# First block's mixers: gated output product with 128 output rows, splits behind chains, rotation on GpSimd, key squares on ScalarE

## The reference, cut to what matters

```python
# layer 0: q, k, v, a_low, r, q_mem = split(h @ gla_w_in); 4 heads, keys 128, values 256, 4 chunks of 64
scores  = einsum('bnhid,bnhjd->bnhij', qc * exp(bc - b_ref), kc * exp(b_ref - bc))     # causal in a chunk
o_intra = einsum('bnhij,bnhjv->bnhiv', scores, vc)
# state before chunk n: S_n = decay * S_(n-1) + (kc * exp(b_last - bc))^T vc,  S_0 = 0
o_inter = einsum('bnhid,bnhdv->bnhiv', qc * exp(bc), s_prev)
o = rmsnorm(o_intra + o_inter, gla_out_norm) * silu(r)
# layer 1: c_q, c_kv, k_r, q_mem = split(h @ mla_w_in)
q  = (rmsnorm(c_q) @ w_uq)  -> q_nope, q_rope;   kv = (rmsnorm(c_kv) @ w_ukv) -> k_nope, v     # 8 heads
q_rope = apply_rope(rmsnorm(q_rope), cos, sin)
# memory, both layers: k, v = split(rmsnorm(mem) @ mem_w_kv); k = rmsnorm(k); softmax attention, 4 heads
x = x + concatenate([o, o_mem]) @ w_out
```

## Time and profile before

| | us |
|---|---|
| median of 3 runs | 1778.82 |
| lowest, highest | 1773.97, 1779.57 |
| the profiled execution | 1773.2 |
| its span, first to last instruction | 1771.4 |

### The profile page before, as it was taken

One profiled execution on the slowest core, in us unless ns is written; L12 is line 12 of the kernel. 1 busy time (PEld: TensorE's weight loads), 2 busy tenths in 40 slices (PEclk: granted clock), 3 DMA queues, 4 the chain that ended last, 5 costly groups with the idle time before them and its releaser, 6 DMA issues.

```text
span 1771.4 us, 28082 instructions
## 1 busy us (share of the span) xinstructions
PE 1687.7 (95%) x10080; PEld 1470.2 (83%) x10080; DVE 1237.3 (70%) x1810; ACT 953.1 (54%) x1548; POOL 73.5 (4%) x78
## 2 busy tenths in 40 slices
PE   7999999899999999999699999997999998899998
PEld 6999987599999989987579899984788877578887
DVE  5876786347766787675766876758577668767765
ACT  5654553446555555555555654547455445755553
POOL 0100010000000000001200100000000001000000
PEclk9999999999999999999999999999999999999999
DMA  6666554244655456544415665550366654037652
GB/s 220 204 208 189 161 166 144 83 163 157 207 185 178 159 197 201 185 159 155 131 54 168 199 204 189 165 186 25 109 199 196 194 180 132 12 119 220 195 192 93
DMA packets 79329, 287.00 MB, mean 162 GB/s; under 512 B 8848, under 2 KB 9232, under 8 KB 79008
## 3 DMA queue, kind: packets, MB, share of 16 engines
q1 hardware_dynamic: 78336, 282.25, 49.6%
q0 software_dynamic: 608, 3.15, 0.5%
q10 hardware_dynamic: 320, 0.74, 0.1%
HBM read 285.05 MB, written 1.05 MB: 162 GB/s over the span
## 4 chain that ended last, share of the span: by engine, by line
PE 82%; DVE 8%; ACT 5%; DMA 3%; issue 2%; POOL 0%; SPq 0%; ACTq 0%; DVEq 0%; POOLq 0%
PE ps L1828 25%; PE ps L1832 13%; PE ps L1755 9%; PE ps L1800 6%; PE ps L1801 6%; PE ps L1802 6%; PE ps L1813 3%; DMA raw<-units 3%; PE ps L1814 3%; PE ps L1815 3%; PE ps L2164 2%; PE ps L2128 2%; DVE wlo L1097 2%; ACT whi L728 1%; PE ps L1915 1%
## 5 line engine op out<-in xcount | busy, mean ns | idle before, releaser
L1261 DVE TENSOR_TENSOR wlo<-raw,whi 128x1024 fp32r<-128x1024 f32 x380 | 463.7, 1223 | 122.7 <-ACT whi L857 122.0
L1828 PE MATMUL ps<-acts,whi 128*128 128x512 f32 x2016 | 505.9, 393 | 1.7 <-DVE prob L1268 1.0
L857 ACT ACTIVATE whi<-raw 128x1024 fp32r<-128x1024 f32 x380 | 398.2, 1051 | 94.8 <-PE ps L1832 63.9
L1828 PEld LDWEIGHTS ps<-acts,whi 128*128 128x128 f32 x2016 | 365.3, 189 | 69.6 <-DVE prob L1268 1.4
L1832 PEld LDWEIGHTS ps<-acts,wlo 128*128 128x128 f32 x2016 | 275.1, 190 | 19.7
L1097 DVE TENSOR_TENSOR wlo<-raw,whi 128x1024 fp32r<-128x1024 f32 x154 | 187.6, 1236 | 135.4 <-ACT whi L728 134.9
L1832 PE MATMUL ps<-acts,wlo 128*128 128x256 f32 x2016 | 281.1, 282 | 0.0
L728 ACT ACTIVATE whi<-raw 128x1024 fp32r<-128x1024 f32 x154 | 159.5, 1054 | 142.0 <-DMA raw<-units 105.7
L1755 PE MATMUL ps<-whi,acts 128*128 128x512 f32 (+1 forms) x708 | 210.5, 389 | 8.7 <-DVE wlo L1097 2.6
L1800 PE MATMUL ps<-hid_hi,wlo 128*128 128x256 f32 x704 | 199.3, 283 | 0.0
L1801 PE MATMUL ps<-hid_hi,whi 128*128 128x256 f32 x704 | 199.3, 283 | 0.0
(11 more groups left out here) (208 smaller groups left out, 2124.1 us busy)
## 6 DMA issues: line engine op xcount, KB each, us to landing
raw<-units SPq DMA_DIRECT2D x534, 512.0 KB, 4.1
arena<-mem_in POOLq DMA_DIRECT2D x2, 1024.0 KB, 7.9
x<-x_in SPq DMA_DIRECT2D x4, 256.0 KB, 6.2
arena<-mem_in POOLq DMA_DIRECT2D x4, 256.0 KB, 4.9
out<-x SPq DMA_DIRECT2D x4, 256.0 KB, 2.1
const<-const_in ACTq DMA_DIRECT2D x1, 560.0 KB, 5.3
row<-row_in ACTq DMA_DIRECT2D x1, 134.0 KB, 6.3
gain<-gain_in SPq DMA_DIRECT2D x1, 76.5 KB, 1.9
```

Source lines behind the costliest of these rows:

```text
L857: nc.scalar.activation(whi[:, u % RING, :], raw[:, u % RAW, :], ACT.Copy).then_inc(hi_ready, 1)
L1261: V.tensor_tensor(wlo[:, u % RING, :], raw[:, u % RAW, :], whi[:, u % RING, :].bitcast(F32), ALU.subtract).then_inc(lo_ready, 1)
L1828: T.matmul(ps[:, bank, :], whi[:, slot, w], acts[:, k].rearrange("p e s -> p (e s)"), start=k == 0, stop=False)
```

## The change

- **Output product.** `g_sT` becomes twice as wide: per token tile a 128x128 matrix with the two chunks' masked scores on its diagonal and zeros beside, written by one longer clearing and two predicated copies of 64 partitions. Each (tile, head) is one full product with v plus products with the states: one in tile 0 (the decayed queries of chunk 0 set to zero), two in tile 1 (queries of the one chunk with zeros for the other). GpSimd clears and copies these queries (`g_qx1`, in the place of the decayed keys once these are transposed); TensorE waits for it (`queries_apart`).
- **Squares and splits.** The product signals after each token tile, and ScalarE squares each at once, with one of its three splits moved behind the squares. The vector engine moves one split behind the gated products, and two behind the q_mem evacuation. The r projection does not wait for the qmT copies. The wait for the gated rows moves from before the memory attention to its first transposes of them.
- **Latent mixer.** Squares of the memory keys on ScalarE, with their sums on the vector engine later; kmT copied by ScalarE rather than the vector engine; the scaling of memory keys and `kn` in another order; rotation of `m_qr` by GpSimd, between the statistics of kn and qn; several splits moved; the latents' transposes two tiles later.

```diff
-SQUARED = {name: TT * (n + 1) for n, name in enumerate(("memq0", "memq1", "kn", "qn", "qr", "bq"))}
+SQUARED = {name: TT * (n + 1) for n, name in enumerate(("memq0", "memq1", "memk1", "kn", "qn", "qr", "bq"))}
...
+        g_sT = at_arena(G_S, 1024).rearrange("p (h t i) -> p h t i", h=GH, t=TT)
+        g_qx = arena3(G_QX, GH, S)
+        g_qx1 = at_arena(G_KD, 1024).rearrange("p (h e i) -> p h e i", h=GH, e=2)
+        QR_OUT = 5 + 6
```

GpSimd in the gated mixer:

```diff
-                    self.stats("memq0", "gla")
+                    self.stats("memq0")
+                    pool.wait_ge(gla_dve, 6)
+                    nc.gpsimd.memset(g_qx[:, :, 0:GC], 0.0).then_inc(queries_apart, 1)
+                    pool.wait_ge(turned, 4)
+                    nc.gpsimd.memset(at_arena(G_KD, 1024), 0.0).then_inc(zeroed, 1)
+                    pool.wait_ge(zeroed, 1)
+                    for e in range(2):
+                        nc.gpsimd.tensor_scalar(g_qx1[:, :, e, e * GC:(e + 1) * GC],
+                                                g_qx[:, :, P + e * GC:P + (e + 1) * GC], 1.0, None, ALU.mult
+                                                ).then_inc(queries_apart, 1)
+                    self.stats("gla")
```

GpSimd in the latent mixer:

```diff
-                    self.stats("memq1", "cq", "ckv", "kr", "memk1", "kn", "qn", "qr")
+                    self.stats("memq1", "cq", "ckv", "kr", "memk1", "kn")
+                    self.rotate_queries()
+                    self.stats("qn", "qr")
+                def rotate_queries(self):
+                    pool.wait_ge(evac_act, QR_OUT)
+                    pool.wait_ge(evac_dve, QR_OUT)
+                    for out_, e, k in ((a, 0, 0), (b, 1, 1), (c, 0, 2), (d, 1, 3)):
+                        tt(out_, v[:, :, :, e, :], tabs[k], ALU.mult).then_inc(rotated, 1)
+                    pool.wait_ge(rotated, 4)
+                    pool.wait_ge(squared, SQUARED["qr"])
+                    tt(v[:, :, :, 0, :], a, b, ALU.subtract).then_inc(rotated, 1)
+                    tt(v[:, :, :, 1, :], c, d, ALU.add).then_inc(rotated, 1)
```

ScalarE in the gated mixer:

```diff
-                    self.split(3)
-                    act.wait_ge(gla_pe, 6)
+                    self.split(2)
                     for t in range(TT):
+                        act.wait_ge(gla_pe, 6 + t)
                         for h in range(GH):
...
+                    self.split(1)
                     self.evacuate(4, vm, NARROW, "mem0")
```

ScalarE in the latent mixer:

```diff
                     self.evacuate(4, km, NARROW, "mem1")
-                    self.memory_keys(1)
+                    act.wait_ge(ss_dve, STAT["memq1"][1])
+                    self.squares_of(square_q, km)
                     self.split(1)
...
                     self.squares_of(rows, m_qn)
+                    self.take([(kmT[:, h, :], GAIN_AT["memk_norm"] + 1) for h in range(XH)])
                     self.split(2)
                     self.evacuate(2, m_qr, MIDDLE, "cq")
-                    self.split(2)
-                    act.wait_ge(ss_dve, STAT["memq1"][1])
+                    self.split(1)
+                    act.wait_ge(ss_dve, STAT["memk1"][1])
                     self.squares_of(square_q, m_qr)
                     self.split(2)
                     self.evacuate(2, m_v, CROSSED, "ckv")
                     self.take([(by_tile(m_krT), None)])
                     self.take([(by_tile(m_kT[:, h, :]), GAIN_AT["mla_kn_norm"]) for h in range(MH)])
-                    self.split(1)
+                    self.split(2)
```

The vector engine in the gated mixer:

```diff
-                        if dst in (G_KJ, G_KD):
-                            self.split(1 if dst == G_KJ else 2)
+                        if dst == G_KJ:
+                            self.split(1)
                     self.evacuate(4, qm, NARROW, "mix0")
-                    self.split(2)
+                    self.split(4)
...
                     self.evacuate(8, g_r, WIDE, "mix0")
-                    self.split(3)
+                    self.split(2)
                     dve.wait_ge(gla_act, 6)
...
                         ins.then_inc(rows_ready, 1)
+                    self.split(1)
                     self.evacuate(4, vm, NARROW, "mem0")
```

The vector engine in the latent mixer:

```diff
                     self.evacuate(4, km, NARROW, "mem1")
-                    self.memory_key_sums(1, rows)
                     self.split(1)
+                    self.evacuate(2, m_k, WIDE, "ckv")
+                    dve.wait_ge(squared, SQUARED["memk1"])
+                    self.sums_of("memk1", square_q, XH)
+                    self.split(1)
+                    dve.wait_ge(squared, SQUARED["kn"])
+                    self.sums_of("kn", rows, MH)
                     self.scale_memory_keys(1)
...
-                    self.evacuate(2, m_k, WIDE, "ckv")
-                    self.split(2)
-                    dve.wait_ge(squared, SQUARED["kn"])
-                    self.sums_of("kn", rows, MH)
+                    self.split(1)
                     self.evacuate(3, m_qn, CROSSED, "cq")
-                    self.memory_keys(1)
-                    self.split(2)
                     kn = m_k.rearrange("p t (h w) -> p t h w", h=MH)
                     self.scale_heads("kn", kn, kn, MH, NOPE).then_inc(rows_ready, 1)
+                    self.g += 2
+                    self.split(2)
                     self.evacuate(2, m_qr, MIDDLE, "cq")
-                    self.split(2)
                     dve.wait_ge(squared, SQUARED["qn"])
...
+                    self.split(1)
                     self.evacuate(2, m_v, CROSSED, "ckv")
-                    self.step(self.rotate(m_qr.rearrange("p t (h e c) -> p t h e c", h=MH, e=2),
-                                          [m_tab[:, 0, n] for n in range(4)], tmp))
-                    self.split(1)
+                    self.split(2)
                     self.g += 1 + 4 + 4
+                    dve.wait_ge(rotated, 6)
                     dve.wait_ge(ratio_ready, 2)
```

TensorE:

```diff
-                    self.project(range(KD), 1024, WIDE, between=beside)
+                    self.project(range(KD), 1024, WIDE, between=beside, taken=False)
                     def read():
+                        pe.wait_ge(queries_apart, 3)
...
-                                for e in range(2):
-                                    n = 2 * t + e
-                                    r = slice(e * GC, (e + 1) * GC)
-                                    o = ps_y[r, t, h * GDV:(h + 1) * GDV]
-                                    ins = T.matmul(o, g_sT[r, h, t, :], g_v[r, t, h * GDV:(h + 1) * GDV],
-                                                   start=True, stop=n == 0)
-                                    if n > 0:
-                                        ins = T.matmul(o, qx[:, h, n * GC:(n + 1) * GC], g_state[:, h, n - 1, :],
-                                                       start=False, stop=True)
-                        ins.then_inc(gla_pe, 1)
+                                w = slice(h * GDV, (h + 1) * GDV)
+                                states = [(qx[:, h, 0:P], 0)] if t == 0 else [(g_qx1[:, h, e], 1 + e) for e in range(2)]
+                                T.matmul(ps_y[:, t, w], g_sT[:, h, t, :], g_v[:, t, w], start=True, stop=False)
+                                for m, (q, n) in enumerate(states):
+                                    ins = T.matmul(ps_y[:, t, w], q, g_state[:, h, n, :], start=False,
+                                                   stop=m == len(states) - 1)
+                            ins.then_inc(gla_pe, 1)
...
-                                 between={1: lambda: latents(0), 3: lambda: latents(1)})
+                                 between={3: lambda: latents(0), 5: lambda: latents(1)})
```

More of the change, by code:

```diff
@@ L412, in build @@
         head_lo = sem("head_lo")
+        zeroed = sem("zeroed")
+        queries_apart = sem("queries_apart")
+        rotated = sem("rotated")
         gla_pe = sem("gla_pe")
@@ L1398, in gla @@
                     dve.wait_ge(gla_dve, 7)
[L1399 removed]
+                    self.step(V.memset(at_arena(G_S, 1024), 0.0))
                     dve.wait_ge(gla_pe, 2)
[L1401 to L1403 removed]
+                    for e in range(2):
+                        r = slice(e * GC, (e + 1) * GC)
+                        mask = constant("tril")[r].bitcast(U32).unsqueeze(1).to_broadcast([GC, 8, GC])
+                        own = g_sT[r].rearrange("p h t i -> p (h t) i")[:, :, e * GC:(e + 1) * GC]
+                        ins = V.copy_predicated(own, mask, ps[r, 5, :].rearrange("p (m i) -> p m i", i=GC))
+                    ins.then_inc(gla_dve, 1)
                     self.split(2)
```

23 lines of the change are left out of this document (12 added, 11 removed).

## The result

| | before | after |
|---|---|---|
| median of 4 runs, us | 1776.88 | 1758.47 |
| lowest, highest | 1773.97, 1779.57 | 1757.61, 1761.47 |
| the profiled execution | 1773.2 | 1761.5 |
| its span | 1771.4 | 1759.7 |

The ratio is 0.9905, with a 95% interval of 0.9889 to 0.9921: about 17 us faster (the two medians lie 18.4 apart), where 19.2 us less than the profiled execution of before, and a median of 1757, were forecast. The total is right; two of its parts are not.

What follows compares the result with a forecast made beforehand. TensorE was taken as the bound, with some 30 us idle, low clock and its own work winnable. Gated 16.5 plus latent 2.7 gave 19.2 us off 1773.2, 1754.0; at the runs' level the median was put at 1757, range 1750 to 1764.

Steps and rivals of the forecast that it cites:

- Query evacuation ahead of splits: Gated mixer: chunk scores start 2.2 us earlier, plus 1.8 us of slow clock won behind them; 4.0 us, bounds 0 and 4.0.
- Rival (c): Gains move into another wait, for weights whose loads stand behind moved splits; 4 us left, no measurable change; chance 0.09.
- qmT copies: Gated mixer: the r projection no longer waits for four qmT copies; gain 1.6 us, bounds 0 and 2.1.
- The product: Gated mixer's output product: 20 full products at 0.43 us, 8.7 us for 13.8; gain 5.1 us.
- Squares: Gated mixer: squares made as each tile ends; wait before the memory attention 5.9 to 1.1 us, gain 4.8, bounds 3 and 5.5.
- Clock in the attention: Gated mixer's memory attention: its first products no longer run at 1.2 GHz; gain 1.0 us.
- GpSimd's work for the product: Gated mixer: clearing and copying queries ends by 280, the product starts at 311.8; costs nothing.
- Latent mixer: Latent mixer: attention 3.2 us sooner with the vector engine ending last, less 0.5 for clock; gain 2.7 us, bounds -5 and +7.
- The latents' 2.6 us: Latent mixer: the wait before the latents' transposes goes, but ScalarE's m_k evacuation gives it all back; bounds 0 and 2.8.
- (a): Latent mixer: GpSimd's rotation ends last by far, 2.6 us a step; total gain 11.9 us, near 1764; chance 0.19.
- (b): Gated mixer: the widened output product costs 0.63 us a product; total gain 15.3 us, near 1761; chance 0.07.
- (d): Latent mixer: each GpSimd rotation step past 5.4 us, making the kernel slower, 1782 us or more; chance 0.05.

Runs made afterwards that it cites:

- run 3: Changed kernel with the vector engine's two splits in front of its half of the q_mem evacuation again; ratio 0.9883 to the kernel before.
- run 10: Changed kernel with the v evacuation ahead of the last split and the two splits in front of the q_mem evacuation again; ratio 0.9907 to the kernel before.
- run 1: Changed kernel with the output product alone put back to 64-row pieces; ratio 0.9934 to the kernel before.
- run 2: Changed kernel with ScalarE's squares behind its third split again, the vector engine's third split ahead of the gated products; ratio 0.9919 to the kernel before.
- run 6: Changed kernel with the latents' transposes at tiles 1 and 3 of the memory projection again; ratio 0.9910 to the kernel before.
- run 11: Changed kernel with the v evacuation ahead of the last split and m_k evacuated before ScalarE's memory-key squares; ratio 0.9884 to the kernel before.

## Why the prediction was right, and where it wasn't

- **Query evacuation ahead of splits, 2.2 + 1.8 us: wrong.** It was worth nothing (run 3). The step that failed is "the splits themselves become 0.7 us later, and so do the loads ...; TensorE eats a unit in 2.73 us and the units are split some 8 us ahead, which hides it". The mask's 1.3 us, covered by the same 8 us, are right in size, and the mask's work stands in the same chain, just ahead of the two splits at 272.82. The margin was reckoned for TensorE's use of the units, and that held: the changed kernel has no wait for a unit in the gated mixer. It wasn't reckoned for ScalarE's evacuation of v, which stands behind the last of these splits. Rival (c) named the place (the loads behind the splits), with 15 us where 2.7 were lost. Before, the same evacuation began at 283.22 right behind TensorE. The 1.8 us of clock were no part of the edit either: with waits of 3.3 and 2.9 us in the same place the next 24 matmuls ran at full clock (runs 3, 10).
- **qmT copies, 1.6 us: right in size.** A to r is 3.0 us shorter in run 3, where the splits' order is that of before. 1.6 are the 24 matmuls behind the chunk scores, which ran at full clock (5.67 us for the 7.27 of the earlier trace rows), and 1.4 remain for the copies; the wait before the r projection itself is 0.4 us there for 2.1. No run changes the copies' wait alone.
- **The product, 5.1 us: right,** 5.2, at 0.43 each (run 1).
- **Squares, 4.8 us: right,** 4.7 in the traces and 4.6 in run 2. The steps hold in detail: from the product's end to the end of the squares 2.0 us (forecast 2.1), of GpSimd's power 4.1 (4.1), of the gated products 7.4 (7.4), of the projection 8.2 (8.5).
- **Clock in the attention, 1.0 us: too small,** 2.3. This 1.3 us more, and the 1.6 us of clock behind the scores, which are luck of the one profile of before, fill most of the hole of 4.0 that the first step left, so the sum of 16.5 met 15.4.
- **GpSimd's work for the product, nothing: right.** It ends at 276, 40 us before its use.
- **Latent mixer, 2.7 us: right in size (2.4); its path holds at one clock and not at the other.** In before's times (13.6 us later than after's) the steps of GpSimd came as forecast: rotation from 851.6 (851.2) to 862.1 (862.7), its statistics to 869.6 (870.3). m_v and the key transposes came 3.6 us sooner (4.0). What failed in the changed kernel's profile is "its memory projection ends at 872.7 for 877.1": it ended at 874.9, at a clock of 0.84 behind the key transposes for 0.91 before, for which the sum had no term. So TensorE ended last and not "the vector engine", which stood 1.30 us for it. In run 3, the same code at a clock of 1.00, it ended at 872.2, TensorE idled 3.3 us (2.8 forecast) and the vector engine ended last, as forecast. The attention starts at the same place in both, so the two chains are nearly level. The clock behind such a wait was priced at 0.5 us; it took 1.7 in run 3 and 1.5 in run 11. The latents' 2.6 us were given back but for up to 1 us, as forecast, though the m_k evacuation alone doesn't explain it (runs 6, 11).
- **Rivals.** (a) twice the time per step: the steps took 1.74 us (1.9 were in the sum), and no run reached 2.6. (b) fell with the 0.43 us a product. (c) came true at its place, for 2.7 us. (d) fell with (a).

Two vector splits beside the rotation took 3.87 us for 2.36, and one GpSimd step 2.19 for 1.28. The Trainium skill, SBUF — State Buffer (Who interferes with whom), states an exclusive lock between the two engines for such instructions; these times agree with it from both sides. In the changed kernel's profile it cost nothing, for neither engine ended last; in runs 3 and 11 GpSimd's chain did.

## What to carry to other kernels

When work in an in-order list is delayed, check the margin of everything that stands behind it in every engine's list and not only of what it makes: TensorE never missed the unit, but the evacuation behind its split had no margin. A gain at one wait must be followed to the next point where the engine waits for the same chain; here the 2.3 us became real only when the evacuation after it was freed as well. Count a wait with the clock around it: a wait taken away can bring more than its length (2.2 us here in the memory attention). And where two chains are nearly level, as in the latent mixer, one profile doesn't tell which of them ends last: a second one, whose clock fell elsewhere, can show the other chain, as run 3 did.

## What the runs showed of the hardware

- After the wait before the r projection the next 12 matmuls took 3.0 to 3.1 us in four profiles (before with a wait of 2.1 us, three with 2.5 to 3.2) and 4.5 to 5.5 us in five (2.0 to 3.7 us); in the five with a wait of 1.0 us or less they took 3.0 to 3.1 every time.
- The same attention code took 57.8 us behind a wait of 5.8 us, at a clock of 0.91, and 54.0 to 55.6 behind one near 1.2, at 0.97 to 1.00.
- In the 18 us behind the start of the key transposes the clock was 0.83 to 0.91 in the twelve kernels where TensorE had waited 2.9 to 6.4 us before them, and 1.00 in the two with 1.6 and 1.7 us (runs 3, 11). Before the latent attention it is those two that waited 3.3 us and lost 1.5 and 1.7 us behind it; twelve with 1.4 to 1.6 us lost nothing.
- Fp32 products of one shape follow each other in 0.43 us; in turns, a pair of 64x64 tiles side by side and a product with 64 output rows cost 0.58 each.
